# A fused encoder block on one core: late query slots at half the pace, and sliding attention in steps a slot apart

## What is computed

```python
# sliding window, per block of 128 rows and 8 heads
scores = einsum('bcqhgd,bckhd->bchgqk', qc, k_band) * HEAD_DIM ** -0.5 - slopes * dist
probs = softmax(concatenate([scores, sink], -1))[..., :-1]
out = einsum('bchgqk,bckhd->bcqhgd', probs, v_band)
...
# PEER, per block of 128 rows
q = (xb @ w_q).reshape(128, 8, 2, 128)
sub_s = einsum('thpc,hpnc->thpn', q, sub_keys)
top_s, top_i = top_k(sub_s, 16)               # 8 heads x 2 halves
cand_s = top_s[:, :, 0, :, None] + top_s[:, :, 1, None, :]
best_s, best_j = top_k(cand_s.reshape(128, 8, 256), 16)
act = gelu(einsum('td,thkd->thk', xb, expert_u[experts]))
out = einsum('thk,thkd->td', softmax(best_s) * act, expert_v[experts])
```

## Time and profile before

| | us |
|---|---|
| median of three executions | 3579.34 |
| the profiled execution, its own time | 3585.65 |
| its span, first to last instruction | 3583.9 |
| start to the first dot product | 410 |
| group 0 gathered (beats 0 to 127) | 972 |
| group 1 gathered (beats 128 to 319) | 1195 |
| group 2 gathered (beats 320 to 511) | 1007 |

### The profile page before, as it was taken

How to read it: one execution, slowest core, us unless ns; L and a number is a source line. 1 busy time by engine, 2 the same in 40 slices (tenths; PEclk the granted TensorE clock), 3 DMA queues, 4 the chain that set the end, 5 groups by cost and what they waited for, 6 DMA issues and landing times.

```text
span 3583.9 us, 40798 instructions
## 1 busy us (share of the span) xinstructions
PE 2282.4 (64%) x13784; PEld 1214.8 (34%) x13784; DVE 2139.1 (60%) x4890; ACT 1110.8 (31%) x3069; POOL 1172.6 (33%) x1033
## 2 busy tenths in 40 slices
PE   7788759988987733888787986664233323333333
PEld 5656634544544411444343542332111111111111
DVE  1111566663647876777667555888666656656654
ACT  2210136533412212666554332212222121112111
POOL 0000123322223233444343423323444434444443
PEclk9889879987998966999897998786665655656565
DMA  6263769985999789999998999988999999999997
GB/s 237 80 247 125 258 264 366 370 339 208 394 391 381 298 330 370 406 417 420 381 417 333 385 389 409 419 356 315 386 421 421 419 384 422 421 402 393 421 419 309
DMA packets 206837, 1265.20 MB, mean 353 GB/s; under 512 B 24778, under 2 KB 30954, under 8 KB 75555
## 3 DMA queue, kind: packets, MB, share of 16 engines
q0 software_dynamic: 147616, 1074.03, 74.4%
q1 hardware_dynamic: 59012, 188.57, 14.5%
HBM read 1247.28 MB, written 15.22 MB: 352 GB/s over the span
## 4 chain that ended last, share of the span: by engine, by line
DMA 29%; DVE 10%; PE 10%; issue 4%; ACT 2%; POOL 0%; DVEq 0%; POOLq 0%; ACTq 0%
DMA ring<-in_uv,idx 29%; PE pb L885 6%; DVE ring L1517 4%; PE pb L811 1%; ACT wts L1146 1%; PE pb L818 1%; DVE kidx L1430 0%; DVE zone L1432 0%; DVE acc L1524 0%; DVE kidx L1436 0%; PE pb L738 0%; DVE vals L1434 0%; ACT gl L1143 0%; ACT L929 0%; POOL ring L600 0%
## 5 line engine op out<-in xcount | busy, mean ns | idle before, releaser
L600 POOL DMA_INDIRECT ring<-in_uv,idx x1024 | 1169.5, 1142 | 2378.7 <-PE pb L885 1779.4
L1517 DVE CUSTOM_DVE_ANT_0 ring<-h2r,ring 128x1024 f32<-128x1024 f32 x1024 | 1235.0, 1223 | 693.3 <-DMA ring<-in_uv,idx 619.4
L885 PE MATMUL pb<-ring,wts 128*32 128x256 f32 x8192 | 754.6, 532 | 1029.9 <-ACT wts L1146 1029.6
L885 PEld LDWEIGHTS pb<-ring,wts 128*32 128x32 f32 x8192 | 310.5, 145 | 1456.1 <-ACT wts L1146 1191.4
L1143 ACT ACTIVATE gl<-dots 128x4 f32<-128x4 f32 x256 | 52.5, 205 | 1490.0 <-DVE dots L1517 1482.8
L929 ACT ACT_TABLE_LOAD x223 | 286.1, 1283 | 4.7 <-PEq L1667 0.7
L1146 ACT ACTIVATE wts<-gm,gl 128x32 f32<-128x32 f32 x1024 | 245.1, 310 | 8.5
L865 PE MATMUL pb<-zone,wst 128*128 128x384 f32 (+1 forms) x768 | 241.0, 469 | 2.3 <-issue 2.3
L865 PEld LDWEIGHTS pb<-zone,wst 128*128 128x128 f32 x768 | 149.4, 200 | 84.1 <-issue 17.8
L811 PE MATMUL pb<-hT,wst 128*128 128x384 f32 x512 | 175.9, 500 | 0.7 <-ACT ys L1060 0.7
L1270 DVE SCALAR_TENSOR_TENSOR zone<-pb,zone 128x384 f32<-128x384 f32 (+2 forms) x120 | 57.2, 476 | 161.7 <-ACT zone L983 153.9
(11 more groups left out here) (173 smaller groups left out, 2586.7 us busy)
## 6 DMA issues: line engine op xcount, KB each, us to landing
wst<-in_w_all SPq DMA_DIRECT2D x148, 512.0 KB
ring<-in_w_all SPq DMA_DIRECT2D x50, 512.0 KB, 10.7
ring<-in_w_ada SPq DMA_DIRECT2D x48, 512.0 KB, 8.7
h2r<-h_scratch SPq DMA_DIRECT2D x128, 128.0 KB
ring<-in_uv,idx POOLq DMA_INDIRECT x1024
ys<-mod_scratch SPq DMA_DIRECT2D x9, 512.0 KB
zone<-in_x SPq DMA_DIRECT2D x8, 512.0 KB, 4.4
hT<-in_x SPq DMA_DIRECT2D x8, 512.0 KB, 15.1
```

What stands on the lines that cost most here:

```text
L600: pool.indirect_dma_start(ring[:, n % RING, :], None, uv, bass.IndirectOffsetOnAxis(ap=idx4[:, piece % 2, col:col + 1], axis=0)).then_inc( ...
L885: m = pe.matmul(pb[32 * f:32 * f + 32, 6 + q // 2, (q % 2) * 256:(q % 2 + 1) * 256], wts[:, n % WBUFS, :], ring[:, n % RING, D + 256 * f:D ...
L1517: dve.tensor_tensor_reduce(u, h2r[:, q, :], u, 1.0, 0.0, ALU.mult, ALU.add, dots[:, n % 16:n % 16 + 1]).then_inc(dots_done, 1)
```

## The change

1. **Late query slots.** The last 12 slots of each mixer's queries (`LATE_QUERIES = 18 - 6`) leave the spread. For mixers 1 and 2 the rest of the plan ends at the same beat as before (107 and 299); the 12 slots then stand in every second beat, from 2 beats after (beats 110, 112, ... 126 for mixer 1), and the last three in the first three beats of the next group (128, 129, 130; 320, 321, 322). Mixer 2 begins at beat 131 instead of 128. The beats 0 to 4 keep their slots.
2. **Sliding attention.** Blocks stand five slots apart, and the steps one slot apart: `take(0)` in k=5, `mix(0)` and `flip(1)` in k=6, `take(1)` in k=7, `mix(1)` and the copy of the result in k=8. A mixer of three blocks has 19 slots, of two 14. ScalarE goes through the blocks of a slot in reverse. Each slot has its own weight (`sw_weight`) instead of 4.0 for all.
3. **Pieces.** The second piece of a group may begin in the group before, so its steps stand one a beat. The second piece of the kernel has its steps two a beat from beat 2, not seven in beat 2.
4. The slot tables are computed once for all groups, and the background is one generator across groups.

By the new table sliding attention of mixer 1 has 19 slots in beats 51 to 66 (15 in beats 48 to 57 before), that of mixer 2 19 in beats 222 to 242 (15 in beats 215 to 227 before). The stages between keep about their beats.

```diff
+SW_STEP = 5
 def sw_slots(g):
-    return 4 * (blocks_of(g) - 1) + 7
+    return SW_STEP * (blocks_of(g) - 1) + 9
+def sw_weight(g, s):
+    pe = dve = act = 0.4
+    for i in range(blocks_of(g)):
+        k = s - SW_STEP * i
+        pe += {0: 4.0, 4: 3.3, 6: 7.0, 8: 3.7}.get(k, 0.0)
+        dve += {1: 4.3, 3: 2.2}.get(k, 0.0)
+        act += {2: 5.5, 5: 1.2, 7: 1.2, 8: 0.6}.get(k, 0.0)
+    return max(pe, 1.5 * dve, 1.2 * act)
...
-LATE_QUERIES = [3, 3, 2, 2, 2]
+LATE_QUERIES = 18 - EARLY_QUERIES
...
+    for g in range(1, NG):
+        w = plan(g)[:-LATE_QUERIES]
+        end = GROUPS[g][0] * HEADS * 8 - LEAD
...
+        for k in range(LATE_QUERIES):
+            begin = end + 2 + 2 * k if k < LEAD // 2 - 1 else end + LEAD + k - LEAD // 2 + 1
+            out[begin] += 1
+        begin += 1
...
-            out.setdefault(max(2 if blk == 0 else 0, first - LEAD + k), []).append((i, k))
+            out.setdefault(2 + k * 7 // 13 if i == 1 else first - LEAD + k, []).append((i, k))
...
                     for s in range(sw_slots(g)):
-                        for i in range(n):
-                            k = s - 4 * i
+                        for i in reversed(range(n)):
+                            k = s - SW_STEP * i
                             if k == 2:
                                 exponentials(i)
-                            elif k == 4:
+                            elif k == 5:
                                 take(i, 0)
-                            elif k == 5:
+                            elif k == 7:
                                 take(i, 1)
-                            elif k == 6:
+                            elif k == 8:
                                 act.wait_ge(ysw_done, 2 * (a + i) + 2)
```

More of the change, by code:

```diff
@@ L186, with slots_at @@
 EARLY_QUERIES = 6
-LATE_QUERIES = [3, 3, 2, 2, 2]
+LATE_QUERIES = 18 - EARLY_QUERIES
 def early_slots():
     return 25 + KT + 2 * blocks_of(0) + 2 + EARLY_QUERIES
[L195 to L210, removed]
+def slots_at():
+    out = [0] * (NB * HEADS * 8)
+    begin = 0
+    for h, k in enumerate((3, 3, 2, 2, 2)):
+        out[h] = k
+        begin = h + 1
+    for g in range(1, NG):
+        w = plan(g)[:-LATE_QUERIES]
+        end = GROUPS[g][0] * HEADS * 8 - LEAD
+        total, done, sofar = sum(w), 0, 0.0
+        for h in range(begin, end):
+            until = total * (h + 1 - begin) / (end - begin)
+            while done < len(w) and sofar + w[done] <= until + 1e-6:
+                sofar += w[done]
+                done += 1
+                out[h] += 1
+        out[end - 1] += len(w) - done
+        for k in range(LATE_QUERIES):
+            begin = end + 2 + 2 * k if k < LEAD // 2 - 1 else end + LEAD + k - LEAD // 2 + 1
+            out[begin] += 1
+        begin += 1
+    return out
 PIECES = [(0, 0, 2), (0, 2, 4), (0, 4, 6), (0, 6, 8)]
@@ L559, in _ @@
                     copies(0, q)
+                background = spans(rest, *(mixer(g) for g in range(1, NG)))
                 for g in range(NG):
                     a, b = GROUPS[g]
-                    background = spans(rest if g == 0 else (), mixer(g + 1)) if g + 1 < NG else None
-                    rate = slots_at(g + 1) if g + 1 < NG else None
                     for blk in range(a, b):
@@ L1181, in _ @@
                     step(0, k)
+                background = spans(rest, *(mixer(g) for g in range(1, NG)))
                 for g in range(NG):
                     a, b = GROUPS[g]
-                    background = spans(rest if g == 0 else (), mixer(g + 1)) if g + 1 < NG else None
-                    rate = slots_at(g + 1) if g + 1 < NG else None
-                    steps = pieces_at(g)
                     for at in range((b - a) * HEADS * 8):
@@ L1197, in _ @@
                             final(blk - 1, 1)
-                        for piece, k in steps.get(at, ()):
+                        for piece, k in steps.get(a * HEADS * 8 + at, ()):
                             step(piece, k)
-                        if background is not None:
-                            for _ in range(rate[at]):
-                                next(background)
+                        for _ in range(rate[a * HEADS * 8 + at]):
+                            next(background)
                 final(NB - 1, 0)
```

36 lines of the change are left out of this document (13 added, 23 removed).

## The result

Four executions of the changed kernel took 3469.32 to 3476.11 us, median 3475.95. Beside them the kernel before has a median of 3586.36 us. The ratio is 0.9684 with a 95% interval of 0.9648 to 0.972: the change takes 3.2% off, by this ratio about 113 us (the medians differ by 110), where I had forecast 46 us. The time lies 9 us under the low end of my range, near rival B.

A forecast was written before the change was run, and what follows sets the result against it. The prediction took idle DMA time, 172 us, as all there was to win, with VectorE full in the queries. Terms 32 + 9 + 6 + 0 + 3 + 1 - 5 = 46 us, from 3579.34 to 3533 us; range 3485 to 3574.

The forecast's parts named there:

- rival B: Whole kernel, 18%: everything opens, the ring lets VectorE lend time, late slots vanish under the gathers; gain 100 us, 3479 us.
- The 172 us of idle DMA: Groups 0 and 1 before the change: DMA engines idle 136 and 36 us, the most the change can win.
- Forecast 32 and 9 us: Sliding attention: idle DMA falls from 44 to 12 us in mixer 1 and from 15 to 6 in mixer 2.
- My sign: Sliding attention of mixer 1: ScalarE's wait for the transposes, 28 us before, gone or under 5 us in all.
- the late queries of mixer 1, 6 us, and of mixer 2, 0 us: Query slots: idle goes from 34 to 28 us in mixer 1, 26 to 28 in mixer 2, taken as 0.
- six query slots keep their share, 4/12 of 27 = 9 us: Queries of mixer 1: six slots, four with tops, stay at about the old density and keep 9 us idle.
- 12.9 us of VectorE against 11.3 us of DMA: Late query slots, over two beats: VectorE still binds by 1.6 us a slot, 19 us for twelve.
- rival D: Late beats, 8%: VectorE binds, queries cost 38 us net; slower by 0.5% if the rest returns under 20 us; 3602 us.
- the other stages, 3 us: Merge, output and stick-breaking get one or two more beats each; 3 of their 34 us idle come back.
- the start of mixer 2, -5 us: Beat 131: ScalarE's first square waits for x, loaded only after mixer 1's tops; loss 5 us, bounds 0 to 15.
- Pieces, 1 us: Piece steps spread: under 1 us at beats 128 and 320, 1 us from moving beat 2's seven steps to beats 2 to 9.
- My signs for the late beats: Beats 108 to 130: VectorE over 0.9 busy, stretch about 150 us, DMA share near 0.88; a share of 1 shows B.

## Why the prediction was too small

**Right: what there was to win.** The 172 us of idle DMA were the whole of it; 100 of the 116 us of shorter span are idle time gone, and the rest is the start and rounding. By the terms of my sum those 100 us are: sliding attention 55 instead of 41, late queries 39 instead of 6, everything else about 6. So the term that failed is the late queries.

**Right in part, too small: sliding attention.** Forecast 32 and 9 us, traced 40 and 15. That the work goes faster with `take` out of the slot of its `flip` fits the runs: undone alone it costs 22 us, with the weights as the open rival. My sign was a wait for the transposes under 5 us; it is 10.9 us, from 28. What failed is the price of density, and in both directions. I had read mixer 2's row at 15 slots in 13 beats as what density gives. The old form in 11 beats idles 16 us in mixer 1, and in 14 beats 5 us in mixer 2, so a beat more brought 24 and 10 us; the wider spacing around the old steps then brought nothing measurable more. Since the room alone or the new form alone takes away most of this idle time, that the 32 us came out near 40 is in part luck: I had put them down to the new form only.

**Wrong: the late queries of mixer 1, 6 us, and of mixer 2, 0 us.** Traced 23 and 16 us; this is 33 of the missing us, and it is where the prediction failed. Two steps of that sum failed. First, "six query slots keep their share, 4/12 of 27 = 9 us": I shared out the idle of the stretch 1165 to 1279 over all slots with tops, but this stretch holds only the twelve slots that move, and the six that stay are the row before it, 1108 to 1165, with a share of 0.98 and 1 us of idle. After the change they idle nothing (1.02). That is 9 us too much in each mixer, read off a row that I had shown. Why four full beats cost nothing is argued, not shown: the ring lets gathers run up to five beats ahead, so only a longer series would starve them. Second, "12.9 us of VectorE against 11.3 us of DMA", an excess of 19 us in twelve slots. VectorE did bind, but both sides of the comparison were low. By my numbers the 23 beats had 23 x 3.2 + 12 x 6.5 = 152 us for VectorE and 23 x 5.0 + 12 x 1.25 = 130 us for the DMA, 22 us apart (19 counted by pairs of beats). The stretch took 163 us with VectorE never waiting for a tile, and the DMA engines were busy 0.93 x 163 = 152 us of it. The difference is 11 us in place of 19. In beats 110 to 130, 155 us, the software queue (the gathers) and the hardware queue (everything else) took, in packets, MB and share:

```profile
q0 software_dynamic: 6458, 46.98, 78.2%
q1 hardware_dynamic: 2640, 7.34, 14.3%
```

That is 121 us for 45 tiles of 1.05 MB, 2.7 us each where the quiet stretch has 2.5, and 22 us for nine weights, sixteen h2 copies of 128 KB and four loads of the sub-keys, 128 KB each; x is not among them. I had named the h2 copies in the bounds and against rival D, but not in the sum. Taken together 9 and 8 us a mixer make up the miss of 33.

**Nearly right by itself, and yet incomplete: "the other stages, 3 us".** In the changed kernel stick-breaking with its projections and merge with output idle 17 and 12 us instead of 19 and 15, so about 5 us came back. Beats 5 to 50 and 67 to 100:

```profile
482.00:766.00 284.00, 250.34 (x1476) 133.72 (x1477) 184.88 (x410) 169.92 (x399) 104.98 (x90) 0.92 0.94 376
869.00:1119.00 250.00, 221.84 (x1092) 117.64 (x1090) 138.26 (x260) 71.60 (x173) 79.87 (x71) 0.93 0.95 380
```

What I did not see is how much the place of twelve heavy slots is worth: the run that keeps it empty loses 48 us, most of it in sliding attention. I counted the beats each stage gets (one or two) and took them for little. In the changed kernel the new form reaches the same idle time of sliding attention, so the 48 us and its 55 us overlap and cannot be added.

**Wrong in sign: the start of mixer 2, -5 us.** I had expected one wait of 5 to 20 us. ScalarE's first square in beat 131 finds x loaded; its wait of 18 us is gone. In the trace after, the three squares follow each other without a wait, and the first of them starts 5 us after the beat began:

```profile
1338.12 1.04 ACT L961 ACTIVATE hT<-zone 128x1024 f32<-128x1024 f32 x1
...
1339.35 1.06 ACT L961 ACTIVATE hT<-zone 128x1024 f32<-128x1024 f32 x1
...
1340.59 1.06 ACT L961 ACTIVATE hT<-zone 128x1024 f32<-128x1024 f32 x1
```

**Pieces, 1 us:** about 8 us, by a run whose interval holds 2 to 15 (its median is 6 us lower). Where they come from is not settled; no stretch of that trace idles over 4 us more or less than before.

**The rivals.** B came out, 3479 us at 18%, and nearly by its own terms: 40 and 13 us in sliding attention (40 and 15), 45 in the queries (39). Its reason failed all the same: it has the late slots vanish under the gathers, and VectorE still binds there, 11 and 10 us of idle stay, and the share is 0.93 and not 1. B also doesn't name the room that the slots leave. That its number is so close is in part luck. D's point of decision was right in kind. At one slot a beat the late slots take 28 us back, and with 2.6 us more in each, 59. My signs for the late beats, VectorE over 0.9 busy and a stretch of 150 us, were off too: 136 of 163 us are busy (0.83), for the time between instructions that follow on each other is not in the busy time. That VectorE was the limit is read from its missing waits and the added work instead.

**The rule of the Trainium skill** ("DMA: Bandwidth & Descriptors", section "Where 436 GB/s comes from") put the limit at about 358 GB/s. The mean over the span is now 364 GB/s and group 1 moves 401, so the trace does not agree here either.

## What to carry to other kernels

Where a background is spread over a loop, heavy slots that are not needed at once are worth moving past the point where the rest must end. Much of the gain can be in the stages that get their room (48 of 76 us here, as long as sliding attention had its old form), so price those by the idle time in their own rows and not by the number of beats, and expect the gain to overlap with any change that makes the same stages cheaper. The way ends where the next stage's room is taken: the same move gave 14 us into a group with nothing behind it, and cost 11 us into one with a mixer behind it. And when idle time is shared out over instructions, first look which of them stand in that row.

## What was new about the hardware

A wait that stands out in the profile need not cost anything: ScalarE waited 72 of 163 us for TensorE in the late beats, and yet a little work added on VectorE in every late slot lengthened each of the two stretches by 32 us and the kernel by 59. With no idle time left, the DMA engines carried 401 GB/s over 1146 us of group 1 while every other engine worked beside them; before, it was 386.
